# The even block's x turned before it is scaled, 1/rms put on behind the products, and a third pair of buffers for the output weights

## Chip, cores, metric

One core of a Trainium2 chip runs the whole program. The metric is the device time of one execution in microseconds (us). TensorE is called PE, VectorE DVE, ScalarE ACT, GpSimd POOL, and SyncE, which issues most DMAs, SP.

## The reference, cut to what matters

Two models of two layers each are chained over x of 256 tokens and 1024 channels, in fp32. The change touches only the first mixer, which begins with

```python
def rms_norm(x, g):
    xf = x.astype(jnp.float32)
    y = xf * lax.rsqrt(jnp.mean(xf * xf, axis=-1, keepdims=True) + EPS)
    return (y * g.astype(jnp.float32)).astype(x.dtype)

def even_mixer(xn, w_in, q_gain, k_gain, sconv_w, w_out):
    proj = xn @ w_in                                   # 1024 x 3072
    q, k, v, gate_b, gate_c, h = jnp.split(proj, ...)  # 512 columns each
    q = rms_norm(heads(q), q_gain); k = rms_norm(heads(k), k_gain)
    a = dilated_attention(q, k, v)
    b = gate_b * causal_dwconv(gate_c * h, sconv_w)
    return jnp.concatenate([a, b], axis=-1) @ w_out    # 1024 x 1024

x = x + even_mixer(rms_norm(x, even_norm[0]), ...)
x = x + conv_glu_ffn(rms_norm(x, ffn_norm[0]), ...)
```

A retention mixer, a second gated feed-forward, a pooling mixer, a mixture of experts, latent attention and a second mixture of experts follow.

## The kernel before

**Blocks.** Each engine runs its own program, block after block: `even_*`, `ffn_*`, `ret_*`, and so on. Tokens are two tiles of 128 (t = 0, 1). In front of each block stands `norm_*`(k), with k = 0 for the even block: squares and sums (ACT for tile 0, L431, and DVE for tile 1, L477), the power -1/2 on POOL (L471), x times 1/rms into `hs` (DVE, L493), 16 transposes of `hs` on PE (L545), and the split of each turned chunk into a high part (ACT, L446, times the gain g) and a low part (DVE, L505). `SPLIT[0]` is the pair `r_x` where both parts go. The transposed x is 8 chunks in 4 banks b, and ACT and DVE work bank by bank.

**Products in three.** Every fp32 operand is a rounded high part and the rest; `three_products` (L726 to L728) multiplies high by high, high by rest and rest by high. Weights come through a ring of 6 slots of 2 MB (`Units`), issued by SP in order; a slot is loaded again once `used` says that its last quarter has been split. A quarter is 128x1024 of weights; `even_rounds` (ACT, L754) writes its high part and `even_rests` (DVE, L761) its rest into one of two pairs of buffers, `e_w[q % 2]`. Rounding quarter q waits until PE is done with quarter q-2:

```python
if q >= 2:
    act.wait_ge(E("q_used"), q - 1)
```

Quarters 0 to 11 are q, k and v (bank 4 + t, then 6 + t, then 4 + t), 12 to 23 gate c, h and gate b in chunks turned the other way (`conv_chunk`), 24 to 31 the output weights. The first unit of weights is loaded in four pieces, one a quarter.

**Order.** `even_act` puts q, k and v away from PSUM (L878 squares for the heads' norm, L879 a copy) after quarters 3, 7 and 11. `even_dve` sums the squares of each head (L937), POOL takes the power (L906, `even_pool`), DVE scales q and k (L944). Then eight heads run through `heads_pe`, `heads_act` and `heads_dve`, with convolution chunks and roundings between them. gate c is put away by ACT (L883) into `gcT`, gate b (L894) into `gbT`; DVE multiplies gate c by h (L969), convolves (`conv3`), and multiplies by gate b (L981). The result is split (L983, L984), and PE needs it from quarter 28 on. Ahead of quarter 31 ACT rounds the first gate weights of the ffn (L1118, `ffn_first_act`), and DVE makes their rest in two parts around quarter 31's (`rest_part`, L1177). `residual_dve` adds the output to x (L697).

**The start.** SP issues both halves of x, then w_in; ACT issues `cst[:, 0:N_FIRST]` (the identity and the constants -1/2) and `params` (gains, taps, routers). `idle(b, n)` (L518) issues n matmuls of the identity by itself, in places where PE would otherwise pause.

Of the kernel before, what the change touches and what calls it, by code (L numbers as in the profile page):

```python
# [142 lines left out]
def build(nc, const, decay_in, band_in, params, rows, x_in, w_in, w_out, wq, wk, wv, wg, wo_r, w_up, w_down, pool_w, w_dkv, w_uk, w_uv,  # L143
# [6 lines left out]
    with ctx:  # L150
# [56 lines left out]
        def spread(col, *shape):  # L207
# [20 lines left out]

        qk_t = area(0, NT, 2 * BANK)
        v_t = area(2048, NT, BANK)  # L230
        qT, kT = area(3072, 4, S), area(14592, 2, 4, S)
        gbT, gcT, zT = area(5120, 4, S), area(6144, 4, S), area(7168, 4, S)
        mix_hi = placed("mix_hi", [P, 8, S], work_at + 4 * 8192, F32R)
# [8 lines left out]
               for i in range(2)]  # L242
        assert 3 * QUARTER <= n_rows and 12544 + QUARTER <= 13568
# [161 lines left out]
        RAW_X = (2,)  # L405

        def scaled_before(k):

            return NT * sum(j not in RAW_X for j in range(k))

        def norm_act(act, link, k, meanwhile=None):
# [17 lines left out]
            if k == 0:  # L429
# [5 lines left out]
            if meanwhile:  # L435
                meanwhile()
            if k == 0:
                act.wait_ge(E("param_in"), 16)
            g = G(NORMS[k])
            for b in (range(4) if k == 6 or k in SPLIT else [1, 3]):  # L440
                act.wait_ge(E("n_tr"), 4 * k + b + 1)
# [19 lines left out]
        def tiles(k):  # L461

            return (1, 0) if k == 0 else (0, 1)

        def norm_pool(pool, k):
            for i, t in enumerate(tiles(k)):
                if k == i == 0:
                    pool.wait_ge(E("ev_small"), 2)
                else:
                    pool.wait_ge(E("n_ms"), NT * k + i + 1)  # L470
                nc.gpsimd.tensor_tensor(rstd[:, t:t + 1], ms[:, t:t + 1], C("minus_half")[:, 0:1],  # L471
                                        ALU.pow).then_inc(E("n_rstd"), 1)

        def norm_dve(dve, link, k, meanwhile=None):
            if k == 0:
                dve.wait_ge(E("first_in"), 16 * (NT + 1))
                link(nc.vector.scalar_tensor_tensor(hs[:, 1, :], x[:, 1, :], 1.0 / D, x[:, 1, :], ALU.mult, ALU.mult, accum_out=ss[:, 1, 0:1]))  # L477
                nc.vector.tensor_scalar(ms[:, 1:2], ss[:, 1, 0:1], EPS, None, ALU.add).then_inc(E("ev_small"), 1)
# [5 lines left out]
            for i, t in enumerate(tiles(k)):  # L484
                if k in RAW_X:
                    break
# [7 lines left out]
            if meanwhile:  # L494
                meanwhile()
            g = G("g_kvin" if k == 6 else NORMS[k])
            if k in SPLIT:
                for b in range(4):
                    if k in RAW_X and b == 0:
# [22 lines left out]
        def norm_pe(pe, k):  # L522
# [15 lines left out]
            for i, t in enumerate(tiles(k)):  # L538
                if k in RAW_X:
# [4 lines left out]
                for c in range(DC):  # L544
                    last = nc.tensor.transpose(turn_bank(k, c // 2)[:, (c % 2) * S + t * P:(c % 2) * S + (t + 1) * P],  # L545
                                               chunk((x if k in RAW_X else hs)[:, t, :], k, c), ident)
# [198 lines left out]

        def even_rounds(act, units, first, end):
            for q in range(first, end):
# [4 lines left out]
                if q >= 2:  # L752
                    act.wait_ge(E("q_used"), q - 1)
                nc.scalar.activation(view(e_w[q % 2][0][:, :], DC, P), even_raw(units, q), ACT.Copy).then_inc(E("q_round"), 1)  # L754
# [3 lines left out]
        def even_rests(dve, units, first, end):  # L758
            for q in range(first, end):
                dve.wait_ge(E("q_round"), q + 1)  # L760
                nc.vector.tensor_tensor(view(e_w[q % 2][1][:, :], DC, P), even_raw(units, q),  # L761
                                        view(e_w[q % 2][0][:, :], DC, P).bitcast(F32), ALU.subtract).then_inc(E("q_split"), 1)
# [5 lines left out]
        def even_pe(pe, units):  # L768
            def quarter(q, *shape):
                pe.wait_ge(E("q_split"), q + 1)  # L770
                return [view(v[:, :], *shape) for v in e_w[q % 2]]
# [36 lines left out]
            idle(0, 6)  # L808
# [54 lines left out]
        def even_act(act, units, link):  # L863
# [7 lines left out]
            norm_act(act, link, 0, lambda: rounds(2))  # L871
# [12 lines left out]
            act.wait_ge(E("ev_small"), 3)  # L884
# [5 lines left out]
            def between(i):  # L890
                if i in (6, 8):
                    b = (i - 6) // 2
                    act.wait_ge(E("q_used"), Q_CONV + 8 + 2 * (b + 1))
                    nc.scalar.activation(gbT[:, 2 * b:2 * b + 2, :], bank(b, 2, S), ACT.Copy).then_inc(E("ev_gb"), 1)  # L894
# [3 lines left out]
            rounds(Q_EVEN - 1)  # L898
            units.n += 1
            ffn_first_act(act, units, 0, GATE)  # L900
            units.n -= 1
            rounds(Q_EVEN)

        def even_pool(pool):
            pool.wait_ge(E("ev_small"), 4)
            nc.gpsimd.tensor_tensor(hrstd, hms, view(C("minus_half"), NT, 2 * A_HEADS), ALU.pow).then_inc(E("hd_rstd"), 1)  # L906

# [9 lines left out]
        def even_dve(dve, units, link):  # L917
# [7 lines left out]
            def meanwhile():  # L925
                dve.wait_ge(E("param_in"), 16)
                nc.vector.tensor_tensor(gqk, G("q_gain"), G("k_gain"), ALU.mult).then_inc(E("ev_small"), 1)
                rests(2)

# [3 lines left out]
            norm_dve(dve, link, 0, meanwhile)  # L933
# [1780 lines left out]
```

## Time and profile before

| | us |
|---|---|
| median of 3 runs | 1749.15 |
| lowest, highest | 1748.06, 1749.19 |
| profiled execution | 1745.97 |
| its span, first to last instruction | 1744.2 |
| PE busy | 1694.5 (97%) |
| DVE busy | 864.7 (50%) |
| ACT busy | 488.5 (28%) |
| POOL busy | 21.4 (1%) |
| even block, to the first transposes of the next norm | 0 to 130.76 |

Times in the trace are counted from the first instruction. Matmuls overlap, so a row's length is not its cost on PE: the distance from one start to the next is. The same holds for back-to-back instructions of ACT and DVE. A bracket at the end of a row says how long the engine had been idle before it and what ended that.

### The profile page before, as it was taken

What the parts mean: (1) busy time and instruction counts of PE and PEld (TensorE: products, weight loads), DVE (VectorE), ACT (ScalarE), POOL (GpSimd) and SP (SyncE); (2) the same over time, 40 slices, a digit from 0 to 9 for tenths busy, and PEclk for the clock granted to TensorE, in tenths of its full rate; (3) what the DMA queues carried; (4) which work ended last, traced back from release to release, by engine and by line L of the source; (5) the groups of instructions that cost most, each with busy time, mean ns of one, the idle gap of its engine ahead of it and who ended that gap; (6) DMA issues with size and microseconds to landing.
All of it is one profiled execution on the core that took longest, in us unless ns stands there. A gap on an engine that the chain in (4) does not pass through costs nothing.

```text
span 1744.2 us, 23689 instructions
## 1 busy us (share of the span) xinstructions
PE 1694.5 (97%) x9686; PEld 1134.6 (65%) x9686; DVE 864.7 (50%) x1532; ACT 488.5 (28%) x747; POOL 21.4 (1%) x31
## 2 busy tenths in 40 slices
PE   7999999999999999999999999999999999999997
PEld 6979999987789999844444444347764444444342
DVE  5778777765668777723323234233652234233233
ACT  5555444444445444310100100013430000001001
POOL 0100000000000000000000000000000000000000
PEclk9999999999999999999999999999999999999999
DMA  9535556564509556899999999998479999999995
GB/s 371 197 117 173 178 183 230 190 200 153 193 24 314 184 176 225 317 369 424 425 425 424 428 425 425 422 418 310 163 310 404 428 425 425 425 425 427 426 420 242
DMA packets 119931, 542.42 MB, mean 311 GB/s; under 512 B 6040, under 2 KB 52256, under 8 KB 91040
## 3 DMA queue, kind: packets, MB, share of 16 engines
q1 hardware_dynamic: 119408, 539.75, 78.5%
q8 instruction: 65, 1.06, 0.3%
q10 hardware_dynamic: 432, 1.39, 0.2%
q14 instruction: 26, 0.21, 0.0%
HBM read 540.07 MB, written 1.05 MB: 310 GB/s over the span
## 4 chain that ended last, share of the span: by engine, by line
PE 82%; DMA 10%; DVE 5%; ACT 1%; issue 1%; SPq 0%; POOL 0%; DVEq 0%; ACTq 0%; POOLq 0%
PE PS L2106 20%; PE PS L726 11%; PE PS L727 11%; PE PS L728 11%; PE PS L2141 10%; DMA ring<-w_up 7%; PE PS L2061 5%; DMA ring<-w_down 3%; PE PS L567 2%; PE PS L2089 1%; PE PS L2090 1%; DVE e_w_lo L761 1%; PE PS L2122 1%; PE PS L1598 0%; PE PS L1052 0%
## 5 line engine op out<-in xcount | busy, mean ns | idle before, releaser
L2106 PE MATMUL PS<-ring,work 128*64 128x512 f32 x1152 | 280.5, 593 | 6.5 <-DMA ring<-w_up 6.5
L2204 DVE SCALAR_TENSOR_TENSOR work<-PS,small,work 128x512 f32<-128x512 f32 x32 | 24.0, 750 | 464.1 <-PE PS L2106 464.1
L2106 PE MATMUL PS<-work 128*64 128x512 f32 x656 | 203.2, 592 | 0.0
L2106 PEld LDWEIGHTS PS<-ring,work 128*64 128x64 f32 x1152 | 91.5, 137 | 169.9 <-issue 168.7
L2141 PE MATMUL PS<-ring,work 128*64 128x512 f32 x576 | 155.9, 595 | 1.6 <-ACT work L2168 1.6
L2162 ACT ACTIVATE work<-PS 128x512 f32<-128x512 f32 x32 | 19.1, 597 | 403.5 <-PE PS L2106 403.5
L2106 PEld LDWEIGHTS PS<-work 128*64 128x64 f32 x656 | 66.2, 137 | 92.2 <-issue 92.1
L2061 PEld LDWEIGHTS PS<-work,hs 128*128 128x128 f32 x1024 | 118.8, 192 | 8.6 <-issue 3.2
L2061 PE MATMUL PS<-work,hs 128*128 128x128 f32 x1024 | 120.1, 276 | 2.7 <-DVE work L2044 2.7
L2141 PE MATMUL PS<-work 128*64 128x512 f32 x368 | 121.3, 595 | 0.0
L1272 DVE TENSOR_TENSOR r_w_lo<-ring,r_w_hi 128x1024 fp32r<-128x1024 f32 x64 | 78.0, 1224 | 59.3 <-ACT r_w_hi L1265 57.9
L2141 PEld LDWEIGHTS PS<-ring,work 128*64 128x64 f32 x576 | 48.7, 137 | 78.8 <-issue 77.8
L2157 ACT ACTIVATE y_hi<-PS 128x512 fp32r<-128x512 f32 x62 | 37.0, 597 | 224.6 <-PE PS L2090 208.9
L1265 ACT ACTIVATE r_w_hi<-ring 128x1024 fp32r<-128x1024 f32 x64 | 67.9, 1065 | 112.4 <-PE PS L728 106.9
L728 PE MATMUL PS<-f_x_hi,f_w_value_lo 128*128 128x256 f32 x352 | 98.8, 281 | 0.0
L726 PE MATMUL PS<-f_x_hi,f_w_value_hi 128*128 128x256 f32 x352 | 98.8, 281 | 0.0
L727 PE MATMUL PS<-f_x_lo,f_w_value_hi 128*128 128x256 f32 x352 | 98.8, 281 | 0.0
L2187 DVE TENSOR_TENSOR x_res<-x_res,PS 128x512 f32<-128x512 f32 x128 | 81.5, 679 | 24.3 <-PE PS L2090 24.3
L726 PE MATMUL PS<-f_x_hi,f_w_gate_hi 128*128 128x256 f32 x320 | 89.9, 281 | 1.3 <-DVE work L1203 1.3
L727 PE MATMUL PS<-f_x_lo,f_w_gate_hi 128*128 128x256 f32 x320 | 89.8, 281 | 0.0
L728 PE MATMUL PS<-f_x_hi,f_w_gate_lo 128*128 128x256 f32 x320 | 89.8, 281 | 0.0
L2181 DVE TENSOR_TENSOR y_lo<-PS,y_hi 128x512 fp32r<-128x512 f32 x62 | 42.8, 691 | 71.8 <-ACT y_hi L2157 71.8
(377 smaller groups left out, 3396.9 us busy)
## 6 DMA issues: line engine op xcount, KB each, us to landing
ring<-w_gate SPq DMA_DIRECT2D x28, 2048.0 KB, 27.0
ring<-w_up SPq DMA_DIRECT2D x28, 2048.0 KB, 26.0
ring<-w_down SPq DMA_DIRECT2D x26, 2048.0 KB, 24.9
ring<-ffn_w_up SPq DMA_DIRECT2D x22, 2048.0 KB, 8.7
work<-w_gate SPq DMA_DIRECT2D x16, 2048.0 KB, 31.1
work<-w_down SPq DMA_DIRECT2D x14, 2048.0 KB, 22.0
ring<-ffn_w_down SPq DMA_DIRECT2D x22, 1024.0 KB, 6.0
work<-w_up SPq DMA_DIRECT2D x10, 2048.0 KB, 22.9
```

Source lines behind the costliest of these rows:

```text
L567: last = nc.tensor.matmul(dst, lhs(c), w(c), start=(c == 0), stop=(c == n - 1))
L726: nc.tensor.matmul(dst, lhs[0], rhs[0], start=start, stop=False, skip_group_check=True)
L727: nc.tensor.matmul(dst, lhs[0], rhs[1], start=False, stop=False, skip_group_check=True)
L728: return nc.tensor.matmul(dst, lhs[1], rhs[0], start=False, stop=stop, skip_group_check=True)
L1265: nc.scalar.activation(r_w[q % 3][0][:, :], raw_quarter(units, q), ACT.Copy).then_inc(E("q_round"), 1)
L1272: nc.vector.tensor_tensor(r_w[q % 3][1][:, :], raw_quarter(units, q), r_w[q % 3][0][:, :].bitcast(F32), ALU.subtract).then_inc(E("q_split" ...
L2061: last = nc.tensor.matmul(bank(GATHER[b])[:, c * P:(c + 1) * P], hs[:, t, (4 * b + c) * P:(4 * b + c + 1) * P], sel[:, t, :], start=(t == ...
L2106: last = nc.tensor.matmul(PS[CAP * e:CAP * (e + 1), what, :], xg[:, c, CAP * e:CAP * (e + 1)], chunk_of(w[e], c), start=(c == 0), stop=(c ...
L2141: last = nc.tensor.matmul(PS[CAP * e:CAP * (e + 1), 2 + n, :], e_hT[:, c, CAP * e:CAP * (e + 1)], part_of(w[e], c)[n], start=(c == 0), sto ...
L2157: nc.scalar.activation(hi[:, :], bank(2 + n), ACT.Copy).then_inc(q["y_hi"], 1)
L2181: nc.vector.tensor_tensor(lo[:, :], bank(2 + n), hi[:, :].bitcast(F32), ALU.subtract).then_inc(q["y_lo"], 1)
L2187: nc.vector.tensor_tensor(v, v, bank(COMBINE[n][t]), ALU.add).then_inc(q["add"], 1)
```

## The change

- **x is turned unscaled.** Norm 0 has no squares, power or scaling ahead of its transposes; they take x itself. The second half of x is issued by ACT in place of `params`, which SP now issues behind the first piece of w_in. ACT and DVE round and rest quarter 0 ahead of the split of x and quarter 1 in its middle (`meanwhile(1)`, `meanwhile(2)`).
- **12 matmuls of a zeroed block** are issued by PE before it waits for x.
- **The squares** of x are taken by ACT after quarter 4's rounding. 1/rms goes on as ACT's scale where q, k and v are put away.
- **Gates.** Two matmuls spread 1/rms over tokens as a row in bank 2 (in place of two of six idle ones); ACT copies the row and its square to `token_rms` and `token_rms_2`; POOL multiplies gate c by the square (which covers h too) and gate b by the row.
- **Output weights** go through three pairs of buffers; the third lies where kT was. The rounding and rest of quarter 31 now come ahead of the ffn's.

```diff
-        RAW_X = (2,)
+        RAW_X, UNSCALED = (2,), (0, 2)
...
-                act.wait_ge(E("first_in"), 16 * (NT + 1))
-                link(nc.scalar.activation(hs[:, 0, :], x[:, 0, :], ACT.Square, accum_out=ss[:, 0, 0:1]))
-                nc.scalar.activation(ms[:, 0:1], ss[:, 0, 0:1], ACT.Copy, bias=EPS, scale=1.0 / D).then_inc(E("n_ms"), NT)
...
+                        if k == 0:
+                            sp.dma_start(par[:, :], params).then_inc(E("param_in"), 16)
...
+        def even_place(q):
+            return e_w[q % 2 if q < Q_OUT else (q - Q_OUT) % 3]
...
-                    act.wait_ge(E("q_used"), q - 1)
+                    act.wait_ge(E("q_used"), q - 1 - (q > Q_OUT + 2))
...
-            idle(0, 6)
+            pe.wait_ge(E("n_rstd"), NT)
+            for t in range(NT):
+                last = nc.tensor.matmul(bank(2)[:, t * P:(t + 1) * P], rstd[:, t:t + 1].to_broadcast([P, P]), ident, start=True, stop=True)
+            last.then_inc(E("tok_ps"), 1)
+            idle(0, 4)
...
+                if n == 0:
+                    rounds(5)
+                    for t in range(NT):
+                        link(nc.scalar.activation(sq[t], x[:, t, :], ACT.Square, accum_out=ss[:, t, 0:1]))
+                        nc.scalar.activation(ms[:, t:t + 1], ss[:, t, 0:1], ACT.Copy, bias=EPS, scale=1.0 / D).then_inc(E("n_ms"), 1)
                 rounds(4 * n + 6)
+                if n == 0:
+                    act.wait_ge(E("n_rstd"), NT)
...
-                        nc.scalar.activation(sq[t][:, n * BANK:(n + 1) * BANK], bank(4 + 2 * n + t), ACT.Square)
-                    nc.scalar.activation(dst, bank(4 + 2 * (n % 2) + t), ACT.Copy).then_inc(E("ev_qkv"), 1)
+                        nc.scalar.activation(sq[t][:, n * BANK:(n + 1) * BANK], bank(4 + 2 * n + t), ACT.Square, scale=rstd[:, t:t + 1])
+                    nc.scalar.activation(dst, bank(4 + 2 * (n % 2) + t), ACT.Copy, scale=rstd[:, t:t + 1]).then_inc(E("ev_qkv"), 1)
+            act.wait_ge(E("tok_ps"), 1)
+            nc.scalar.activation(token_rms, bank(2, S), ACT.Copy).then_inc(E("ev_tok"), 1)
+            nc.scalar.activation(token_rms_2, bank(2, S), ACT.Square).then_inc(E("ev_tok"), 1)
...
-            rounds(Q_EVEN - 1)
-            units.n += 1
-            ffn_first_act(act, units, 0, GATE)
-            units.n -= 1
-            rounds(Q_EVEN)
+            rounds(Q_EVEN)
+            ffn_first_act(act, units, 0, GATE)
...
+            pool.wait_ge(E("ev_tok"), 2)
+            for i, (gates, by) in enumerate(((gcT, token_rms_2), (gbT, token_rms))):
+                for b in range(2):
+                    pool.wait_ge(E("ev_gc"), 2 * i + b + 1)
+                    v = gates[:, 2 * b:2 * b + 2, :]
+                    nc.gpsimd.tensor_tensor(v, v, by.unsqueeze(1).to_broadcast([P, 2, S]), ALU.mult).then_inc(E("ev_scaled"), 1)
...
-            sp.dma_start(x[:, 1, :], x_in[0, P:S, :]).then_inc(E("first_in"), 16)
...
+            pe.wait_ge(E("ev_small"), 1)
+            for _ in range(12):
+                nc.tensor.matmul(bank(7, P), blank, blank, start=True, stop=True)
...
-            act.dma_start(par[:, :], params).then_inc(E("param_in"), 16)
+            act.dma_start(x[:, 1, :], x_in[0, P:S, :]).then_inc(E("first_in"), 16)
```

## Rows read from the trace of the kernel before

**Rows 1.** Timeline of the start: start us, us, engine, line, what [idle before]

```profile
7.45 1.06 ACT L431 ACTIVATE hs<-x_res 128x1024 f32<-128x1024 f32 x1 [4.28 <-DMA x_res<-x]
...
8.80 1.04 ACT L754 ACTIVATE e_w_hi<-ring 128x1024 fp32r<-128x1024 f32 x1
10.13 1.06 ACT L754 ACTIVATE e_w_hi<-ring 128x1024 fp32r<-128x1024 f32 x1 [0.29 <-DMA ring<-even_w_in]
10.43 3.42 PE L545 MATMUL PS<-tables,hs 128*128 128x128 f32 x16 [10.43 <-DVE hs L493]
12.89 3.03 ACT L446 ACTIVATE f_x_hi<-PS,tables 128x256 fp32r<-128x256 f32 x8 [1.70 <-PE PS L545]
13.88 3.23 DVE L505 SCALAR_TENSOR_TENSOR r_x_lo<-PS,tables,f_x_hi 128x256 fp32r<-128x256 f32 x8 [0.44 <-PE PS L545]
16.46 0.39 PE L779 MATMUL PS<-e_w_hi,f_x_hi 128*128 128x512 f32 x1
19.22 0.40 PE L779 MATMUL PS<-e_w_hi,f_x_hi 128*128 128x512 f32 x1
```

**Rows 2.** Timeline of ACT, quarters 5 and 6, and PEld's start of quarter 6

```profile
25.00 1.06 ACT L754 ACTIVATE e_w_hi<-ring 128x1024 fp32r<-128x1024 f32 x1 [1.67 <-PE PS L784]
25.96 0.58 ACT L878 ACTIVATE work<-PS 128x512 f32<-128x512 f32 x1
...
27.87 1.08 ACT L754 ACTIVATE e_w_hi<-ring 128x1024 fp32r<-128x1024 f32 x1
...
30.26 0.19 PEld L726 LDWEIGHTS PS<-e_w_hi,f_x_hi 128*128 128x128 f32 x1 [0.18 <-DVE e_w_lo L761]
```

**Rows 3.** Timeline of DVE around quarter 10

```profile
39.17 1.22 DVE L937 TENSOR_REDUCE small<-work 128x16 f32<-128x1024 f32 x1 [0.72 <-ACT work L879]
40.42 1.22 DVE L761 TENSOR_TENSOR e_w_lo<-ring,e_w_hi 128x1024 fp32r<-128x1024 f32 x1
```

**Rows 4.** Timeline of PE in the output product, starts of quarters 28 and 31

```profile
114.87 0.50 PE L726 MATMUL PS<-e_w_hi,mix_hi 128*128 128x512 f32 x1 [0.34 <-DVE e_w_lo L761]
123.26 0.50 PE L726 MATMUL PS<-e_w_hi,mix_hi 128*128 128x512 f32 x1 [1.25 <-DVE e_w_lo L761]
```

**Rows 5.** Chain that ended last, 0 to 140 us: start us, us, what

```profile
118.91 1.91 ACT f_w_gate_hi L1118
130.76 1.77 PE PS L545 x16
```

**Rows 6.** DMA issues begun at 1.20 (x), 1.67 (ring), 1.19 (params): KB, us to landing

```profile
x_res<-x SPq DMA_DIRECT2D x1, 512.0 KB, 6.1
ring<-even_w_in SPq DMA_DIRECT2D x1, 512.0 KB, 7.1
tables<-params ACTq DMA_DIRECT2D x1, 509.5 KB, 6.3
```

**Rows 7.** The same view, issues between 4.05 and 4.1 us

```profile
ring<-even_w_in SPq DMA_DIRECT2D x1, 2048.0 KB, 14.2
```

**Rows 8.** Groups of POOL by line, whole span: busy us, mean ns

```profile
L471 POOL TENSOR_TENSOR small<-small,tables 128x1 f32<-128x1 f32 x18 | 10.8, 601 | 1512.5 <-ACT small L427 954.4 <-ACT small L1572 452.8 <-ACT small L1886 93.7
L906 POOL TENSOR_TENSOR small<-small,tables 128x32 f32<-128x32 f32 x1 | 5.4, 5438 | 34.2 <-DVE small L939 34.2
```

**Rows 9.** Groups of ACT by line and shape, 0 to 130 us: busy, mean ns

```profile
L887 ACT ACTIVATE work<-PS,small 128x512 f32<-128x512 f32 x2 | 1.3, 686 | 0.0
```

**Rows 10.** Timeline of the gates: ACT lays them down, DVE takes them

```profile
62.20 0.58 ACT L883 ACTIVATE work<-PS 128x512 f32<-128x512 f32 x1
77.64 0.68 DVE L969 TENSOR_TENSOR work<-work,PS 128x512 f32<-128x512 f32 x1
97.29 0.59 ACT L894 ACTIVATE work<-PS 128x512 f32<-128x512 f32 x1
102.48 0.59 ACT L894 ACTIVATE work<-PS 128x512 f32<-128x512 f32 x1
108.58 1.22 DVE L981 TENSOR_TENSOR work<-work 128x1024 f32<-128x1024 f32 x1
```

More of the change, by code:

```diff
@@ L226, in build @@
         lg = scratch(208, NT, N_ROUTE)
+        blank = area(0, P)
         qk_t = area(0, NT, 2 * BANK)
@@ L242, in build @@
                for i in range(2)]
+        e_w += [[placed(f"e_w2_{part}", [P, QUARTER], work_at + 4 * (14592 + QUARTER * j), F32R) for j, part in enumerate(("hi", "lo"))]]
         assert 3 * QUARTER <= n_rows and 12544 + QUARTER <= 13568
@@ L404, in build @@
         SHARED = (1, 2, 3, 4)
-        RAW_X = (2,)
+        RAW_X, UNSCALED = (2,), (0, 2)
         def scaled_before(k):
-            return NT * sum(j not in RAW_X for j in range(k))
+            return NT * sum(j not in UNSCALED for j in range(k))
         def norm_act(act, link, k, meanwhile=None):
@@ L428, in norm_act @@
                                          scale=1.0 / D).then_inc(E("n_ms"), 1)
-            if k == 0:
-                act.wait_ge(E("first_in"), 16 * (NT + 1))
-                link(nc.scalar.activation(hs[:, 0, :], x[:, 0, :], ACT.Square, accum_out=ss[:, 0, 0:1]))
-                nc.scalar.activation(ms[:, 0:1], ss[:, 0, 0:1], ACT.Copy, bias=EPS, scale=1.0 / D).then_inc(E("n_ms"), NT)
             if k == 8:
                 return
-            if meanwhile:
+            if meanwhile and k:
                 meanwhile()
             if k == 0:
+                meanwhile(1)
                 act.wait_ge(E("param_in"), 16)
@@ L440, in norm_act @@
             for b in (range(4) if k == 6 or k in SPLIT else [1, 3]):
+                if k == 0 and b == 2:
+                    meanwhile(2)
                 act.wait_ge(E("n_tr"), 4 * k + b + 1)
@@ L461, in tiles @@
         def tiles(k):
-            return (1, 0) if k == 0 else (0, 1)
+            return range(NT)
         def norm_pool(pool, k):
             for i, t in enumerate(tiles(k)):
[L467 to L470, printed above, removed]
+                pool.wait_ge(E("n_ms"), NT * k + i + 1)
                 nc.gpsimd.tensor_tensor(rstd[:, t:t + 1], ms[:, t:t + 1], C("minus_half")[:, 0:1],
@@ L498, in norm_dve @@
                 for b in range(4):
+                    if k == 0 and b == 2:
+                        meanwhile(2)
                     if k in RAW_X and b == 0:
@@ L752, in even_rounds @@
                 if q >= 2:
-                    act.wait_ge(E("q_used"), q - 1)
-                nc.scalar.activation(view(e_w[q % 2][0][:, :], DC, P), even_raw(units, q), ACT.Copy).then_inc(E("q_round"), 1)
+                    act.wait_ge(E("q_used"), q - 1 - (q > Q_OUT + 2))
+                nc.scalar.activation(view(even_place(q)[0][:, :], DC, P), even_raw(units, q), ACT.Copy).then_inc(E("q_round"), 1)
                 if q % 4 == 3:
@@ L760, in even_rests @@
                 dve.wait_ge(E("q_round"), q + 1)
-                nc.vector.tensor_tensor(view(e_w[q % 2][1][:, :], DC, P), even_raw(units, q),
-                                        view(e_w[q % 2][0][:, :], DC, P).bitcast(F32), ALU.subtract).then_inc(E("q_split"), 1)
+                nc.vector.tensor_tensor(view(even_place(q)[1][:, :], DC, P), even_raw(units, q),
+                                        view(even_place(q)[0][:, :], DC, P).bitcast(F32), ALU.subtract).then_inc(E("q_split"), 1)
                 if q % 4 == 3:
@@ L770, in quarter @@
                 pe.wait_ge(E("q_split"), q + 1)
-                return [view(v[:, :], *shape) for v in e_w[q % 2]]
+                return [view(v[:, :], *shape) for v in even_place(q)]
             def first_quarter(w, k):
@@ L932, in even_dve @@
                 nc.vector.memset(kT[other, i, :, :], 0.0)
-            norm_dve(dve, link, 0, meanwhile)
+            norm_dve(dve, link, 0, rests)
+            nc.vector.tensor_tensor(gqk, G("q_gain"), G("k_gain"), ALU.mult).then_inc(E("ev_small"), 1)
             rests(10)
@@ L985, in even_dve @@
             dve.wait_ge(E("ev_conv"), 1)
-            rests(Q_EVEN - 1)
-            rest_part(dve, 0, GATE, 0, units.slot(1), 0)
             rests(Q_EVEN)
-            rest_part(dve, 0, GATE, 0, units.slot(), 1)
+            for part in range(2):
+                rest_part(dve, 0, GATE, 0, units.slot(), part)
             residual_dve(dve, "even", first_bank=4)
@@ L1308, in ret_pe @@
                                                     start=True, stop=True)
-                        last.then_inc(E("rt_tok_ps"), 1)
+                        last.then_inc(E("tok_ps"), 1)
                     continue
@@ L2637, in _ @@
             units = Units(dve)
+            nc.vector.memset(blank, 0.0)
             nc.vector.memset(small[:, 428:429], 0.0).then_inc(E("ev_small"), 1)
```

31 lines of the change are left out of this document (12 added, 19 removed).

## The prediction

> **What bounds the kernel now.** I read the page first: TensorE (PE) is busy nearly the whole span, so what counts is time in which it has nothing to do or runs slowly. Then I read the waits of PE over the span, the chain of waits for the first 140 us, the timelines of each engine there, and last the DMA issues. The change touches only the even block, the first 127 us; everything later follows from when that block ends, because its loads wait for ring slots which earlier work frees. A microsecond won here is a microsecond at the end, as long as nothing in the block gives it back.
>
> Four places in the block matter. (a) The start: x is there at 7.4, but PE turns it from 10.43, after squares, 1/rms and scaling, and it needs 3.42 for 16 transposes. Quarter 1 of the products starts at 16.46, quarter 2 at 19.22, so a quarter lasts 2.76 [rows 1]. (b) The loop round, rest, products has two buffers and no slack: quarter 6 is rounded the moment ACT has put the first products away (27.87), and PE's weight load then waits 0.18 for the rest [rows 2]. DVE's sum of squares waits for ACT to put the k products away, and the rest of quarter 10 stands right behind it [rows 3]. (c) In the output product PE waits for the rest of quarter 28 (0.34 in the row) and of quarter 31 (1.25) [rows 4]. Quarter 31 is late because ACT rounds ffn weights from 118.91 for 1.91 ahead of it [rows 5]. (d) The attention heads between them are bound by DVE and are not touched, save that POOL now works beside them.
>
> **The change part by part.** *Turning x as it lands.* Two squares, two powers and two scalings leave the path between x and the transposes. What takes their place is DMA. Before, 512 KB of x, 512 KB of w_in, 509.5 KB of params share the start, and landed at 1.20 + 6.1 = 7.3, 1.67 + 7.1 = 8.8, 1.19 + 6.3 = 7.5 [rows 6]. Now x's second half takes params' place on ACT's queue and params stand behind quarter 0 on SP's. The sizes are alike, so x and quarter 0 should be there by about 7.4, and params when the same bytes have passed as before quarter 0's landing: 8.8. Quarter 1 has the same bytes ahead of it as before: ACT waited for it until 10.13 [rows 1].
> From there I step forward. ACT rounds quarter 0 at 7.45 to 8.5, DVE makes its rest by 9.8. PE turns x from 7.45; if the clock is up, in the 1.77 of a later norm [rows 5], done at 9.25. ACT needs params: 8 high parts took 3.03, 0.36 from start to start, so banks 0 and 1 (four) last 8.8 to 10.25; then it rounds quarter 1 to 11.3. DVE's low parts go at 0.39 each [rows 1] from 9.8, so the rest of quarter 1 runs 11.35 to 12.6. PE: quarter 0 from 9.85 to 12.65, quarter 1 from 12.7. DVE's last four low parts and the rest of quarter 2 end at 12.6 + 1.6 + 1.2 = 15.4, just as PE gets there at 15.46. Before it was 16.46: gain 3.75. An earlier x would not help, since quarter 1's landing sets this.
> The next bound is the second unit of w_in. It lands at 4.07 + 14.2 = 18.3 [rows 7], behind the same bytes as before. Quarter 4's rounding would now like to start at 18.5; it just fits. The later units have slack of microseconds.
>
> *The 12 blank matmuls.* They run from about 1.2, before x is there. The 16 transposes took 0.21 each at 10.43 and 0.11 each at 130.76 [rows 1, 5]: half speed (1.2 GHz) and full (2.4). The clock rose while x was being turned, with nothing but those transposes before it. Twelve blank matmuls, two records each at 0.21, put up to 5 us of such work ahead of x, more than 3.42; so I take the transposes at 1.77. The other bound is 3.42.
> The Trainium skill ("TensorE: Matmul & The Clock Gate", What's actually happening) says that the first stretch after idleness runs at half clock whatever is issued, and that its end varies from run to run. By it the clock would be up at x here too, with some luck; were it not, the sum is that of the rival below.
>
> *Squares moved behind quarter 4's rounding, on ACT.* One square with its small copy takes 8.80 - 7.45 = 1.35 [rows 1], two take 2.7. ACT's hole there is the 1.67 before 25.00, plus 0.1 [rows 2]: 2.7 - 1.77 = 0.93 late. Behind it stand quarter 5's rounding, its rest and PE, which have no slack: lose 0.93. The powers (0.60 each [rows 8]) come before ACT is through quarter 5's rounding, with some 0.1 to spare.
>
> *1/rms put on by ACT.* With a scale taken from memory a 128x512 copy takes 0.686 [rows 9] instead of 0.58 [rows 2]. Four such instructions for q stand ahead of quarter 6, four for k ahead of DVE's sum and quarter 10: 0.4 + 0.4 lost. Those for v lie in a pause of ACT. The two copies for token rows and the two matmuls that spread rstd (in place of two idle ones) lie there too: 0. If that pause were gone they would cost 0.8.
> The Trainium skill ("ScalarE: Activation LUTs", What ACT_TABLE_LOAD costs) gives some 93 ns for each scale or bias read from memory. The row's 0.11 agrees; by the page the two terms would sum to 0.75.
>
> *Four products on POOL.* No row shows a plain multiply there. A lower bound is DVE's: 1.22 for 128x1024 [rows 10], so 0.6 for 128x512. The upper one is POOL's power, 0.60 for one column and 5.44 for 32 [rows 8]: 0.156 a column, 80 us for 512. A multiply is no power; I take the fixed 0.6 and DVE's 0.6, 1.2 together. Gates c are there at 62.8 and wanted at 77.6, gates b at 97.9 and 103.1 and wanted at 108.58 [rows 10]: hidden by 4 us at 1.2. Beside them DVE may run slower, for POOL reads and writes the same memory: nothing at best, all four lengths (4.8) at worst; only the second and the third lie beside DVE work that sets PE's time, and mostly beside instructions that read PSUM. I take 0.2.
> The Trainium skill ("GPSIMD Engine Reference", Performance versus the Vector engine) finds a two-input add about twice as slow as on DVE: an estimate of 1.3 each by it, the same sum.
>
> *Three pairs of buffers.* From quarter 27 rounding runs one further ahead. Quarter 27 is rounded at once behind 26, so DVE makes its rest without waiting and comes to the convolution's split and quarter 28's rest sooner; I take the wait of 0.34 [rows 4] and the restart behind it as gone: 0.4. ACT now rounds quarter 31 directly after 28 is done and the ffn weights come after, so its rest is there 1.5 us before PE: its whole wait goes. Two and a half quarters behind 114.87 end at 121.8, so that is 123.26 - 121.8 = 1.4 [rows 4]. Gain 1.8. The ffn rests then end some 0.5 us before or about when the first residual add wants DVE, as before; the last add waits for PE.
>
> Sum: 3.75 - 0.93 - 0.8 - 0.2 + 1.8 = 3.6; I round to 3.5 for the power's thin margin. The profiled execution took 1745.97 (span 1744.2); that becomes 1742.5. The runs shown have a median of 1749.15, 3.2 above the profiled one, as another 1.1 lies between themselves; the change is taken off the median: 1745.6.
>
> **The rivals.**
> *The squares and scales cost nothing* (ACT catches up before PE feels it). Against it stands the wait of 0.18 [rows 2]; for it only that the two waits are inferred. Gain 5.2: 1743.9.
> *The clock is still low when x is turned.* The transposes end 1.65 later (10.9), DVE's first low parts wait for them and push both rests: gain at quarter 2 is 2.4, in all 2.1: 1747.0.
> *POOL and DVE hold each other up.* DVE stands still during the two products beside its path: 2.4 instead of 0.2. Gain 1.3: 1747.8.
> *The start is bound by DMA.* The new order lets the second unit of w_in land some 2 us late, or params after 10; only the output part stays: gain 1.8 - 0.2, with 0.4 of the start, 2.0: 1747.2.
> *Slower: POOL's multiply is slow.* The last gates must be there by 108.6, the first of them starts at 97.9. Two products of p each end at 97.9 + 2p: late from p = 5.3, the gain of 3.5 is gone at p = 7.1, and at p = 10, an eighth of the power's slope, DVE's split and quarter 28 are 9.4 late: 1755.
>
> **How the numbers follow.** Chances: forecast 0.52, squares free 0.13, clock low 0.10, POOL against DVE 0.10, DMA 0.08, POOL slow 0.07. 0.2% of 1749.15 is 3.5 us, about what a measurement of this kernel can tell from no change, and the forecast sits on that edge: half of its cases lie above. Faster by more: 0.26 + 0.13, and some of the others, whose prices I may have put too high: 0.46. Slower: 0.06. Within: 0.48. The range takes in the free squares and a microsecond of scatter below (1742.8) and the cases up to no gain (1749.3) above; the forecast's own is 1744.2 to 1747.2.
>
> **What would show each step.** Transposes of L545's successor begin at 7.5 at 0.11 each; quarter 1 starts at 12.7; a wait of about 0.9 before quarter 5 and of 0.4 before 6 and 10; POOL products near 1.2; the first ffn transposes at 130.6 - 3.5 = 127.1; and no wait before quarters 28 and 31. Wrong would be a product of POOL above 5 us, DVE instructions grown longer beside it, transposes at 0.21, or an ACT that waits for DMA at quarter 4.

## The result, and the profile after

| | before | after |
|---|---|---|
| median, us | 1750.55 (22 runs) | 1753.3 (22 runs) |
| lowest, highest | 1746.98, 1756.3 | 1750.01, 1758.54 |
| ratio, 95% interval | | 1.0015 [1.0008, 1.0022] |

The kernel became about 2.7 us slower where 3.5 us faster was forecast, and its time lies above the range. The forecast missed the change by some 6 us, in size and in sign, although a loss this small is within the 0.2% that was called no change. The time itself is 7.7 us above the forecast's 1745.6, and 1.4 of that is the kernel before: 1749.15 in three runs, 1750.55 in 22. The profile after is that of the slowest of the 22 executions (1758.54). Yet the part of the kernel that was changed did nearly what the prediction says. This is the start, on all engines, by start, length, engine and line, with the idle time before it:

```profile
5.71 0.85 PE L2589 MATMUL PS<-work 128*128 128x128 f32 x3
...
7.31 2.01 PE L542 MATMUL PS<-tables,x_res 128*128 128x128 f32 x16 [0.75 <-DMA x_res<-x]
7.46 1.06 ACT L757 ACTIVATE e_w_hi<-ring 128x1024 fp32r<-128x1024 f32 x1 [4.27 <-DMA ring<-even_w_in]
...
9.83 0.50 PE L782 MATMUL PS<-e_w_hi,f_x_hi 128*128 128x512 f32 x1 [0.50 <-DVE e_w_lo L764]
...
10.19 1.08 ACT L757 ACTIVATE e_w_hi<-ring 128x1024 fp32r<-128x1024 f32 x1
...
12.70 0.39 PE L782 MATMUL PS<-e_w_hi,f_x_hi 128*128 128x512 f32 x1
...
15.46 0.41 PE L782 MATMUL PS<-e_w_hi,f_x_hi 128*128 128x512 f32 x1
```

x is turned from 7.31 at the full clock (2.01 for 16 where [rows 1] have 3.42), and quarters 1 and 2 of the products start at 12.70 and 15.46, the two figures of the prediction; [rows 1] have 16.46 and 19.22. The same block further on, ACT around the squares and POOL to the next norm:

```profile
18.53 1.06 ACT L757 ACTIVATE e_w_hi<-ring 128x1024 fp32r<-128x1024 f32 x1 [1.75 <-PE PS L787]
19.49 1.05 ACT L883 ACTIVATE work<-x_res 128x1024 f32<-128x1024 f32 x1
...
22.04 1.04 ACT L757 ACTIVATE e_w_hi<-ring 128x1024 fp32r<-128x1024 f32 x1
22.99 0.67 ACT L892 ACTIVATE work<-PS,small 128x512 f32<-128x512 f32 x1
...
25.27 1.07 ACT L757 ACTIVATE e_w_hi<-ring 128x1024 fp32r<-128x1024 f32 x1
```
```profile
42.18 5.44 POOL L920 TENSOR_TENSOR small<-small,tables 128x32 f32<-128x32 f32 x1 [19.41 <-DVE small L955]
54.91 1.78 POOL L926 TENSOR_TENSOR work<-work 128x512 f32<-128x512 f32 x1 [7.29 <-ACT work L900]
60.54 1.85 POOL L926 TENSOR_TENSOR work<-work 128x512 f32<-128x512 f32 x1 [3.85 <-ACT work L900]
95.66 1.28 POOL L926 TENSOR_TENSOR work<-work 128x512 f32<-128x512 f32 x1 [33.26 <-ACT work L911]
100.86 1.29 POOL L926 TENSOR_TENSOR work<-work 128x512 f32<-128x512 f32 x1 [3.92 <-ACT work L911]
123.41 0.55 POOL L470 TENSOR_TENSOR small<-small,tables 128x1 f32<-128x1 f32 x1 [21.26 <-ACT small L430]
125.32 0.61 POOL L470 TENSOR_TENSOR small<-small,tables 128x1 f32<-128x1 f32 x1 [1.37 <-ACT small L430]
```

Quarter 6 is rounded at 25.27 for 27.87 in [rows 2]. The last row is the mark by which all kernels below are compared, norm 1's second power. Before it stood at

```profile
129.56 0.60 POOL L471 TENSOR_TENSOR small<-small,tables 128x1 f32<-128x1 f32 x1 [1.57 <-ACT small L427]
```

so 4.2 us are won there. A single execution tells this to about a microsecond: in a second trace of the kernel before, this power starts at 130.85, since PE's granted clock rises to 2.4 GHz at 16.0 us there and at 13.5 in the first.

The same powers of norms 2, 3 and 4 and of the router (726.99 before, 723.23 after) show a lead of 3.8 still at 723 us. At the end of the first mixture of experts nothing of it is left, for two reasons that have to be kept apart. The first is scatter: from 723 us to the last product of that block (1177.09 before, 1178.76 after) the lead of 3.8 turns into a lag of 1.7, and on the way the granted clock was 1.2 GHz for 6.8 us at 730 and again at 1099 in this execution, and nowhere in the one before. In the second traces of both kernels that product starts at 1182.18 (before) and 1174.13 (after), with the changed kernel 8 us ahead. The second reason is the same in both traces of the changed kernel, and stands right behind this product. PE there, before and after, in the same timeline:

```profile
1177.09 0.40 PE L2090 MATMUL PS<-y_end_lo,wT 128*128 128x512 f32 x1
1178.06 2.04 PE L1861 MATMUL PS<-tables,x_res 128*128 128x128 f32 x16 [0.58 <-DVE x_res L2187]
```
```profile
1178.76 0.39 PE L2105 MATMUL PS<-y_end_lo,wT 128*128 128x512 f32 x1
1184.16 3.68 PE L1876 MATMUL PS<-tables,x_res 128*128 128x128 f32 x16 [5.01 <-issue]
```

The second trace of the changed kernel:

```profile
1174.13 0.39 PE L2105 MATMUL PS<-y_end_lo,wT 128*128 128x512 f32 x1
1179.45 3.33 PE L1876 MATMUL PS<-tables,x_res 128*128 128x128 f32 x16 [4.93 <-issue]
```

L1861 and L1876 are the same 16 transposes of latent attention. "issue" means that no semaphore and no DMA that the profile knows held them. They are the first ones behind a branch, at the end of the mixture of experts, over code for rare overflow tokens:

```python
pe.br_cond(count <= CAP, on_true=f"moe_pe_done{l}", on_false=f"moe_pe_more{l}").branch_hint(likely)
```

The traces also record PE's branch instruction itself: it starts at 1176.28 and lasts 0.48 before, and starts at 1177.98 and lasts 6.12 after. So PE's program stands in the branch. Behind it the transposes run at half clock. The stretches of both kernels around this place (PE busy, granted clock as a share of 2.4 GHz, DMA share, GB/s):

```profile
1174.00:1185.00 11.00, 9.69 (x47) 1.00 1.02 406
```
```profile
1178.00:1192.00 14.00, 8.99 (x38) 0.76 0.91 364
```

The DMA view, narrowed to the time ahead of the branch, tells what is missing. PE's instructions come by a queue of their own (q8), 16384 bytes in a packet. Before, 1165 to 1178 us:

```profile
q1 hardware_dynamic: 999, 5.38, 101.2%
q8 instruction: 1, 0.02, 0.5%
```

After, 1165 to 1181 us, and then 1181 to 1183:

```profile
q1 hardware_dynamic: 1379, 6.43, 101.0%
```
```profile
q1 hardware_dynamic: 247, 0.80, 100.9%
q8 instruction: 1, 0.02, 3.4%
```

Before, one packet starts at 1171.5, 6.5 us ahead of the transposes. After, none comes between 1148.4 and 1181.5, and PE stands until 1.5 us after that one has landed. The Trainium skill ("Runtime: NRT & Kernel Launch", Instruction fetch mechanics) says that fetching runs ahead in sequence in blocks of 16 KiB, and that a branch to a block not held makes the engine wait for a transfer; the rows agree, with 5.0 us for the wait, which the page does not price. Nothing that the diff does is in that place. What it does to PE's program is to add the 12 blank matmuls: each is two matmul records and two weight loads (9686 and 9710 records of each kind in the two traces), 48 instructions, by which all code behind stands further on.

### The profile page after: what moved, and what is told of

It is laid out like the page before. It is cut to its first block, busy times and chain, and to the rows that moved or that the text cites. A ratio compares the mean times of both kernels' runs of the same rounds, so it can differ in the third digit from the quotient of the medians.

```text
span 1756.7 us, 23743 instructions
## 1 busy us (share of the span) xinstructions
PE 1710.2 (97%) x9710; PEld 1145.4 (65%) x9710; DVE 862.6 (49%) x1528; ACT 491.5 (28%) x752; POOL 27.4 (2%) x35
## 4 chain that ended last, share of the span: by engine, by line
PE 88%; DMA 5%; DVE 4%; ACT 2%; issue 1%; POOL 0%; DVEq 0%; SPq 0%; ACTq 0%
PE PS L2121 23%; PE PS L2156 12%; PE PS L725 11%; PE PS L726 11%; PE PS L727 11%; PE PS L2076 6%; DMA ring<-w_up 4%; PE PS L564 2%; PE PS L2104 2%; PE PS L2105 1%; PE PS L2137 1%; DVE e_w_lo L764 1%; PE PS L1613 0%; PE PS L1930 0%; PE PS L1067 0%
## 5 line engine op out<-in xcount | busy, mean ns | idle before, releaser
L2121 PE MATMUL PS<-ring,work 128*64 128x512 f32 x1152 | 285.4, 603 | 7.7 <-DMA ring<-w_up 7.7
L2156 PE MATMUL PS<-ring,work 128*64 128x512 f32 x576 | 155.9, 595 | 1.6 <-ACT work L2183 1.6
```

What stands on the lines that cost most here:

```text
L2121: last = nc.tensor.matmul(PS[CAP * e:CAP * (e + 1), what, :], xg[:, c, CAP * e:CAP * (e + 1)], chunk_of(w[e], c), start=(c == 0), stop=(c ...
L2156: last = nc.tensor.matmul(PS[CAP * e:CAP * (e + 1), 2 + n, :], e_hT[:, c, CAP * e:CAP * (e + 1)], part_of(w[e], c)[n], start=(c == 0), sto ...
```

## The experiments

All ratios are to the kernel before, timed beside them. Stall is the idle time before the first transposes behind the first mixture of experts, norm 1 the start of its second power in the profiled execution.

| run | median | ratio, 95% interval | norm 1 | stall |
|---|---|---|---|---|
| before, copy | 1750.58 | 1.0002 [0.9993, 1.0011] | 130.85 | 0.59 |
| after, copy | 1752.33 | 1.0012 [1.0, 1.0024] | 125.55 | 4.93 |
| before, three pairs alone | 1748.36 | 0.999 [0.9981, 0.9998] | 128.97 | 0.58 |
| after with two pairs | 1755.15 | 1.0029 [1.0016, 1.0043] | 127.59 | 5.16 |
| after, no blanks | 1745.8 | 0.9975 [0.9965, 0.9984] | 126.84 | 0.60 |
| before with the blanks | 1757.79 | 1.0042 [1.0029, 1.0055] | 130.45 | 5.03 |
| after, 3 wide blanks | 1746.35 | 0.9983 [0.9973, 0.9993] | 125.28 | 0.59 |
| after, 6 blanks | 1747.88 | 0.9991 [0.9981, 1.0001] | 126.21 | 0.59 |
| after, 12 idle matmuls fewer at norm 1 | 1747.47 | 0.9979 [0.9968, 0.9991] | 125.80 | 0.59 |
| before with 96 waits | 1756.07 | 1.0033 [1.0022, 1.0044] | 129.07 | 5.04 |
| before with 512 waits | 1768.17 | 1.0099 [1.0084, 1.0115] | 147.92 | 0.57 |
| 3 wide blanks, no scale | 1744.38 | 0.9963 [0.995, 0.9977] | 124.63 | 0.59 |

**Which part brings the loss.** The first four runs: both kernels once more, and the third pair of buffers by itself and taken away.

The kernel before, unchanged:

> The kernel before, unchanged, for a second trace of it and the granted clock of every run. Theory A (the even block keeps its gain of 4 us and the changed kernel loses more later, in half-clock stretches and in one 5 us stall of PE ahead of the MLA block that the first trace of before does not have): granted clock near 0.995 in most runs, no stall ahead of the MLA block's transposes, time ratio 1.000. Rival B (the later losses are the scatter of any run, and the two profiled executions were a lucky and an unlucky one): clock near 0.992 as in the changed kernel, and such stalls here too.

The changed kernel, unchanged:

> The changed kernel, unchanged. Theory A: 2 to 3 us slower than before again (ratio 1.0015), clock near 0.992, first transposes of norm 1 some 4.2 us earlier than in before, and the 5 us stall of PE ahead of the MLA block's transposes again. Rival B: the stall is absent and the ratio falls anywhere between 0.998 and 1.002.

The kernel before with the third pair and the order of quarter 31 alone:

```diff
+        def even_place(q):
+            return e_w[q % 2 if q < Q_OUT else (q - Q_OUT) % 3]
...
-                    act.wait_ge(E("q_used"), q - 1)
+                    act.wait_ge(E("q_used"), q - 1 - (q > Q_OUT + 2))
...
-            rounds(Q_EVEN - 1)
-            units.n += 1
-            ffn_first_act(act, units, 0, GATE)
-            units.n -= 1
-            rounds(Q_EVEN)
+            rounds(Q_EVEN)
+            ffn_first_act(act, units, 0, GATE)
```

> Before with the third pair of buffers and the new order of the ffn's first weights alone; x, 1/rms, DMAs and PE's program as before. By the sum of the prediction norm 1 starts 1.8 us earlier. Theory A1 (a shorter even block by itself brings the later losses, since everything behind it is shifted against something that stays): slower than 1.8 us gain, ratio 1.000 or above. Theory A2 (the loss comes with what the change adds to PE's program or to the start, not with the shift): ratio 0.999, 1.8 us faster.

The changed kernel with this undone:

> The changed kernel with the output weights back in two pairs and the old order of the ffn's first weights: only the start, the scaling by 1/rms and POOL's products are left of the change. Norm 1 starts some 2.4 us earlier than before. A1: the later loss is smaller or another than in the changed kernel, as the shift is another. A2: the later loss is the same 6 us, so the kernel is 4 us slower than before (ratio 1.002) and 1.8 us slower than the changed kernel.

The copies repeat both kernels, the stall with the one and not with the other. Their granted clocks hardly differ (0.994 and 0.993 in the mean), so neither rival B nor a clock that is lower throughout explains the loss. The third pair wins what was expected (norm 1 is 1.9 earlier than in the copy, where the clock rises as late, 16.0 against 16.3) and brings no stall; without it the stall stays. An earlier end of the even block is therefore not what costs the time: the loss goes with the rest of the change, which is the start, the scales and POOL's products.

**The blank matmuls, taken away, put in, made shorter.** In the expectations "theory L" is that the place of PE's code decides whether the instructions behind the branch come in time; rival R is that the loads, waits or buffers of the even block do. The changed kernel without the blanks:

```diff
-            pe.wait_ge(E("ev_small"), 1)
-            for _ in range(12):
-                nc.tensor.matmul(bank(7, P), blank, blank, start=True, stop=True)
```

> The changed kernel without the 12 blank matmuls and the clearing of their block. They are 24 matmul records and 24 weight loads at the head of PE's program. Theory L (the place of PE's code): with these 48 instructions gone everything behind them stands where it stood in the kernel before; the instruction fetch some 8 us ahead of the branch behind the first mixture of experts is back, the 5.0 us in which PE issues nothing in front of the 16 transposes are gone, and so is the half-clock stretch there. x is turned at half clock, so norm 1 comes about 1.6 us later than in the changed kernel (its last power near 127, against 129.6 before): about 1748, ratio 0.9985 to 0.9995. Rival R (the stall comes from the changed loads, waits or buffers of the even block): the 5.0 us stay and 1.6 us of the start are lost too: ratio 1.002 to 1.003.

The kernel before with these three lines, and the clearing of the block, alone:

> The kernel before with the 12 blank matmuls alone, in front of PE's wait for x (PE waits there until 10.4 us anyway, so they cost no time where they stand and may bring the transposes to full clock, up to 1.6 us). Theory L: the stall of 5 us in front of the first transposes behind the first mixture of experts appears in a kernel in which nothing else was changed, with a half-clock stretch of 3.4 to 6.8 us behind it: 4 to 6 us slower by then, 1753 to 1756 where the kernel before has 1750, ratio 1.002 to 1.0035. Rival R: no stall there, ratio 0.999 to 1.000.

Three blanks of 512 columns:

```diff
-            for _ in range(12):
-                nc.tensor.matmul(bank(7, P), blank, blank, start=True, stop=True)
+            for _ in range(3):
+                nc.tensor.matmul(bank(7), blank[:, 0:P], blank, start=True, stop=True)
```

> The changed kernel with 3 blank matmuls of 512 columns in place of 12 of 128: the same columns, but 12 instructions of PE where there were 48. Theory L: with most of the shift gone there is no stall behind the first mixture of experts, and the clock is up when x is turned as with 12: the whole gain of the even block reaches the end, about 1746, ratio 0.997 to 0.998. Rival R: the stall of 5 us stays, ratio 1.001 to 1.002 as the changed kernel.

Six of 128 columns (`range(6)`):

> The changed kernel with 6 blank matmuls of 128 columns, half of the shift (24 instructions of PE). Theory L: the stall in front of the transposes is all or nothing, near 5 us or none, with ratio 1.001 or 0.998; which of them says between which counts the edge lies. A stall of 2 to 3 us would speak against it (it would then grow with the instructions). Rival R: the stall is 5 us, ratio 1.001 to 1.002.

Theory L holds in all four. Without the blanks the transposes follow at once:

```profile
1174.72 0.39 PE L2104 MATMUL PS<-y_end_lo,wT 128*128 128x512 f32 x1
1175.71 0.49 PE L1875 MATMUL PS<-tables,x_res 128*128 128x128 f32 x2 [0.60 <-DVE x_res L2201]
```

and in the kernel before, with the blanks and nothing else, they do not:

```profile
1180.28 0.39 PE L2091 MATMUL PS<-y_end_lo,wT 128*128 128x512 f32 x1
1185.70 3.68 PE L1862 MATMUL PS<-tables,x_res 128*128 128x128 f32 x16 [5.03 <-issue]
```

That kernel was slower by more than expected (7.8 us by the medians). Its blanks end at 6.2 and x is turned only from 10.00, again at half clock, so they brought nothing there and cost nothing, by norm 1 (130.45, between the two traces of before). The rest lies behind the stall: in its profiled execution the clock is at 1.2 GHz for 20.5 us between 1183 and the end of its work, in the copy of before for 6.8. Over the same part of the program the five traces with the stall have 13.7 to 20.5 us at 1.2 GHz, of which 3.4 or 6.8 stand directly behind it, and the nine without have 3.4 to 10.2. Whether it is the stall that leads to the later ones was not settled. With 3 wide blanks the stall is gone and norm 1 is as early as with 12. The stall is whole or absent: 0, 12 and 24 more instructions have none, 48 have 5.0 us (4.93 to 5.16).

One number came out otherwise. No blanks was expected at 1748 and is at 1745.8, level with the wide ones (1746.35), though its norm 1 is 1.6 us later. x is turned at half clock there:

```profile
7.04 3.65 PE L541 MATMUL PS<-tables,x_res 128*128 128x128 f32 x16 [7.04 <-DMA x_res<-x]
```

So the blanks win 1.6 us in the block, and no run shows them at the end. Two medians whose intervals are 1.6 to 1.8 us to either side could hide that much.

**Is it their work or their place in the code?** The changed kernel with all 12 blanks, but with as many idle matmuls fewer ahead of norm 1:

```diff
-        IDLE = {1: (0, 14), 3: (0, 7), 4: (4, 8)}
+        IDLE = {1: (0, 2), 3: (0, 7), 4: (4, 8)}
```

> The changed kernel with its 12 blank matmuls at the start, and 12 of the 14 idle matmuls ahead of norm 1's transposes taken out: from there on PE's code stands where it stood before. Theory L (the place of the code behind the branch): no stall of 5 us in front of the first transposes behind the first mixture of experts, an instruction fetch some 8 us ahead of them; PE idles for some 3 us at norm 1 instead, where the clock may fall once for 3.4 us, up to 1.7 lost: ratio 0.997 to 0.999. Rival W (work of the blank matmuls at the start, or the clock that they raise, brings the stall by another way): stall of 5 us, ratio 1.001 to 1.002.

The kernel before with instructions that do no work:

```diff
+            for _ in range(96):
+                pe.wait_ge(E("ev_small"), 1)
             pe.wait_ge(E("first_in"), 16 * (NT + 1))
```

> The kernel before with 96 waits for a semaphore that is long there, in front of PE's wait for x. Two waits go into one instruction, so they are 48 instructions, as many as the 12 blank matmuls have, and no work. Theory L: the stall of 5 us is there and the clock falls behind it, 4 to 8 us slower than before, ratio 1.002 to 1.0045. Rival W: no stall, ratio 1.000.

The same with `range(512)`:

> The kernel before with 512 such waits, 256 instructions: by 64 bytes each exactly one of the 16384-byte packets in which instructions are fetched. The start will be later by what 256 instructions take beyond 10.4 us of waiting (0 to 15 us, to be read from the first transposes of x). Theory L in the form 'what counts is where the branch target lies within a packet': the picture of the kernel before comes back, no stall behind the first mixture of experts, and fetches at the same distances from the branch as before. In the form 'anything behind a certain length of program is late': the stall is there, as with 48.

The rival to theory L is here called W: it is the work of the blanks, or the clock that they raise, that brings the stall. The first two runs decide for the place. With the blanks at the start and the code behind norm 1 where it had been:

```profile
1178.44 2.04 PE L1876 MATMUL PS<-tables,x_res 128*128 128x128 f32 x16 [0.59 <-DVE x_res L2202]
```

With 48 instructions that are only waits, already met:

```profile
9.94 3.47 PE L545 MATMUL PS<-tables,hs 128*128 128x128 f32 x16 [9.94 <-DVE hs L493]
...
1184.20 3.45 PE L1861 MATMUL PS<-tables,x_res 128*128 128x128 f32 x16 [5.04 <-issue]
```

The start is not disturbed, norm 1 is even 0.5 earlier than in the profiled execution of before, and the kernel is 5.5 us slower. The third puts five times as many in and the stall is gone:

```profile
28.86 3.31 PE L545 MATMUL PS<-tables,hs 128*128 128x128 f32 x16 [28.86 <-issue]
...
1197.38 2.04 PE L1861 MATMUL PS<-tables,x_res 128*128 128x128 f32 x16 [0.57 <-DVE x_res L2187]
```

Its time is lost at the start alone (18.4 us, more than the 15 allowed for: an instruction with two waits takes 28.86 / 256 = 0.11 us). A shift by 256 instructions changes nothing behind the branch; a shift by 48 does. So what counts is where code lies within a packet, not how long the program is. That 256 instructions fill one packet is what the Trainium skill ("Runtime: NRT & Kernel Launch", Instruction fetch mechanics) says. This run agrees: its trace has 256 more semaphore instructions of PE than that of the kernel before (604 for 348), and 66 packets on q8 for 65. The trace of the run before it has 48 more (396), and 65 packets.

The second mixture of experts ends with the same kind of branch, and it bears this out the other way round. PE's branch instruction there lasts 2.8 to 4.0 us in the six traces with a shift of 0 or 256 instructions (2.78 in the kernel before, 2.79 with 512 waits), and no packet starts in the 19 us ahead of it. It lasts 0.4 to 0.5 in the eight traces with a shift of 12, 24 or 48, with a packet 6.9 to 9.4 us ahead. PE has no matmul left to issue behind that branch, and the span ends 10.2 to 10.3 us after the branch begins in all of them: this late fetch costs nothing.

**The price of the scale.** With `scale=rstd[:, t:t + 1]` taken off the squares and copies of q, k and v (the products are then not normalized), beside the kernel with 3 wide blanks:

```diff
-                        nc.scalar.activation(sq[t][:, n * BANK:(n + 1) * BANK], bank(4 + 2 * n + t), ACT.Square, scale=rstd[:, t:t + 1])
-                    nc.scalar.activation(dst, bank(4 + 2 * (n % 2) + t), ACT.Copy, scale=rstd[:, t:t + 1]).then_inc(E("ev_qkv"), 1)
+                        nc.scalar.activation(sq[t][:, n * BANK:(n + 1) * BANK], bank(4 + 2 * n + t), ACT.Square)
+                    nc.scalar.activation(dst, bank(4 + 2 * (n % 2) + t), ACT.Copy).then_inc(E("ev_qkv"), 1)
```

> The changed kernel with 3 wide blank matmuls, and with 1/rms left out where q, k and v are put away (no scale from memory; the output is then another). It sizes the term of 0.8 us. If the scale costs 0.1 on each of eight instructions that stand ahead of quarters 6 and 10: quarter 6's rounding is 0.4 earlier, quarter 10's 0.8, norm 1 0.8 earlier against the kernel with 3 wide blanks: ratio 0.9978 where that has 0.9983. Rival: the loop catches up before PE feels it, then nothing at norm 1.

Norm 1 is 125.28 - 124.63 = 0.65 earlier. With the scale and without it, the first of the four instructions and the rounding of quarter 6 behind them:

```profile
22.93 0.67 ACT L892 ACTIVATE work<-PS,small 128x512 f32<-128x512 f32 x1
...
25.20 1.07 ACT L757 ACTIVATE e_w_hi<-ring 128x1024 fp32r<-128x1024 f32 x1
```
```profile
22.97 0.58 ACT L892 ACTIVATE work<-PS 128x512 f32<-128x512 f32 x1
...
24.88 1.08 ACT L757 ACTIVATE e_w_hi<-ring 128x1024 fp32r<-128x1024 f32 x1
```

2.27 against 1.91: 0.09 for each instruction. The price reaches norm 1; nothing catches it up. The ratio, 0.9963, is lower than the 0.9978 expected, by more than 0.65 us explain (0.9983 with the scale, less 0.0004); the intervals of the two kernels overlap, and only the trace sizes this term.

## Why the prediction was wrong

**The step that failed** is in its first paragraph: "A microsecond won here is a microsecond at the end, as long as nothing in the block gives it back", with its premise that the change touches only the first 127 us. Without the stall it about holds: the four kernels with the changed start and no stall at the branch (no blanks, moved, wide blanks, six blanks) win 2.7 to 4.3 us at norm 1, against the first trace of before, and 1.6 to 4.4 us at the end, by ratios of 0.9975 to 0.9991. One by one the two do not follow each other (no blanks wins least at norm 1 and most at the end), and the interval of six blanks takes in no gain. It doesn't hold for the instruction stream. The twelve blanks were priced by their time alone (up to 5 us, ahead of x), and the 48 instructions that they are were not counted as a shift of all that follows. The price of the shift can be read between two kernels with the same 12 blanks at the start: 1.0015 with the stall, 0.9979 with the code moved back, so 0.0036, 6.3 us, with some 2.4 to either side by the two intervals. The stall itself is 5.01 - 0.59 = 4.4; the transposes behind it take 3.68 for 2.04, 1.6 more; together 6.0. No rival named it, and the one that ended slower put the loss on POOL.

With the stall away the forecast was about right: "moved" is 0.9979, which on 1749.15 makes 1745.5, for 1745.6 predicted. That agreement is partly luck: the ends of its interval are 2 us to either side, and its block won 3.8 or 5.1 at norm 1, by which trace of before is taken, for the 3.5 of the sum.

**Turning x as it lands: right.** Gain to quarter 2 forecast 3.75, measured 19.22 - 15.46 = 3.76, and the clock was up. x was turned a little earlier than assumed (7.31 for 7.45) and slower (2.01 for 1.77), which was hidden, as PE waited 0.50 for the rest of quarter 0. The kernel before has its own scatter here: in its second trace, with the later clock, quarter 2 starts at 20.44, and the gain against that is 5.0.

**Squares: 0.93 forecast.** Two squares took 22.04 - 19.49 = 2.55 for 2.7, so 0.15 of it was not lost.

**Scale: 0.8 forecast, 0.65 measured** by the last run.

**POOL: right where it mattered.** 1.2 was taken for a product; two took 1.28 and 1.29 and were hidden. The first two took 1.78 and 1.85, 0.50 and 0.56 more, each with a rest of DVE over its first 0.64 and 0.71:

```profile
54.32 1.23 DVE L764 TENSOR_TENSOR e_w_lo<-ring,e_w_hi 128x1024 fp32r<-128x1024 f32 x1 [2.03 <-ACT e_w_hi L757]
...
60.02 1.23 DVE L764 TENSOR_TENSOR e_w_lo<-ring,e_w_hi 128x1024 fp32r<-128x1024 f32 x1 [1.56 <-ACT e_w_hi L757]
```

DVE's length did not change (1.22 or 1.23 without POOL as well), so where the two overlapped POOL was the one that took longer. The fast products were not all alone: DVE was busy for 1.20 of the 1.28 at 95.66, with shorter instructions, and for 0.04 at 100.86. The slow pair also works on other buffers than the fast one, and no run separates that from the overlap. From the heads' power to norm 1 it is 125.32 - 42.18 = 83.14 in the changed kernel and 128.97 - 45.84 = 83.13 with three pairs alone, without any product on POOL: the 0.2 taken for contention was 0.0. The changed kernel with two pairs says the same, 127.59 - 42.45 = 85.14 against the 85.12 of the copy of before. The Trainium skill's ratio of two ("GPSIMD Engine Reference", Performance versus the Vector engine) gave 1.3, and two rows agree.

**Three pairs: 1.8 forecast.** The copy of before needs 130.85 - 45.73 = 85.12 for that stretch, with three pairs 83.13: 2.0. PE has no wait in the output product any more. The kernels' times point the same way, 0.999 added to before and 1.0029 against 1.0012 when taken from after, though the last two intervals overlap.

In all: 2.3 up to the heads' power (44.50 to 42.18; 2.0 by the forecast's terms) and 1.9 behind it, 4.2 for 3.5. Against the copy of before, whose clock rose later, it is 3.55 and 1.98. The kernel before scatters by 1.2 us here from one execution to the next, so the sum is confirmed to about a microsecond and no better.

**What stays open.** Why a shift of 24 instructions keeps the early fetch and one of 48 loses it. The kernel has a hint for the branch ahead of the last down products. The traces record it: it runs 10.6 to 10.9 us ahead of the branch in all fourteen, so it is issued in both cases. Where the fetch is in time a packet starts 5.8 to 6.1 us after it, where it is late only 3.3 to 3.7 us after the branch has begun. The missing packet may be the one that the hint asks for, but no run moved the hint or left it out. It was not found either why the 1.6 us of a warm start are not seen at the end.

## What to carry to other kernels

An instruction costs its place in the program too. Where a kernel branches, compare the wait in front of the branch's target before and after any edit, however far ahead of it the edit is: "issue" before the first instructions there and no q8 packet in the microseconds ahead mean a late fetch, and a few dozen instructions more or fewer before it (48 here) tell whether it is that. A kernel can have several such branches, and one placement need not suit all: here 12 or 24 more instructions had both fetched in time, 0 and 256 only the first, 48 only the second. If PE's clock is to be warmed, few wide matmuls (3 of 512 columns) do it with fewer instructions than many narrow ones. Of the versions that compute the whole reference the changed kernel without the blanks had the lowest time, 0.9975 [0.9965, 0.9984], and the one with 3 wide blanks cannot be told from it.

## What was not expected of the hardware

- The first matmuls behind a branch waited 5.0 us (4.93 to 5.16 in five traces of four kernels) when no 16384-byte packet had been fetched in the microseconds ahead, and 0.6 otherwise. The packet started 3.3 to 3.7 us after the branch had begun, took 1.1 us to move, and some 1.5 us more passed until the first transpose; the time ahead of it and behind it is not explained by the trace.
- PE's clock was at 2.4 GHz ahead of that wait. The 16 transposes behind it ran at 1.2 GHz for most or all of their time and took 3.3 to 3.7 us for 2.04.
- Twelve blanks ending 0.8 us ahead of x left the clock up for it; in the kernel before they ended 3.8 us ahead of the transposes (10.00), which took 3.65 again.
- POOL's product of 128x512 took 1.28 where DVE was all but idle or in short instructions, and 1.78 to 1.85 where a DVE subtraction of 128x1024 lay over its first 0.64 to 0.71; the subtraction kept its 1.23.
